# Recurrence's triangular inverse: products and copies of 32 instead of 64 columns from level 2 on

## The reference

```python
def step(state, inp):
    r_t, w_t, k_t, v_t, kk_t, a_t = inp
    sa = jnp.einsum('bhvk,bhk->bhv', state, kk_t)
    state = (state * w_t[:, :, None, :]
             - sa[..., None] * (kk_t * a_t)[:, :, None, :]
             + v_t[..., None] * k_t[:, :, None, :])
    return state, jnp.einsum('bhvk,bhk->bhv', state, r_t)
```

## Time and profile before

| | |
|---|---|
| median of 3 runs | 2653.7 us (2653.07 to 2654.84) |
| profiled execution | 2649.62 us, of which its span 2647.8 us |
| PE busy | 2543.0 us (96%), 18915 records |
| PE weight loads busy | 2117.9 us (80%) |
| DVE, ACT busy | 1655.8 us (63%), 1355.3 us (51%) |
| mean granted TensorE clock | 0.989 of full speed |
| recurrence of layer 0 | about 309 to 437 us of the span |
| recurrence of layer 1 | about 1088 to 1217 us of the span |

### The profile page before, as it was taken

The page is one execution under the profiler, slowest core; times in us unless marked ns, Lnnn a source line. Parts: engine busy times, 40 slices in busy tenths (PEclk is TensorE's granted clock), DMA queues, the critical chain, the costliest instruction groups (busy, mean ns, idle before and its releaser), DMA issues.

```text
span 2647.8 us, 46804 instructions
## 1 busy us (share of the span) xinstructions
PE 2543.0 (96%) x18915; PEld 2117.9 (80%) x18915; DVE 1655.8 (63%) x1905; ACT 1355.3 (51%) x1605; POOL 58.4 (2%) x94
## 2 busy tenths in 40 slices
PE   8999889999999999989999999988999999998998
PEld 6888577888888887577888888756998998876996
DVE  5546646765555556646765555687876776556774
ACT  5435434644444444334546445475674764456663
POOL 0002000000000002000000000000000000000000
PEclk9999999999999999999999999999999999999999
DMA  6547744645445449544555444402545555542453
GB/s 220 190 183 254 264 145 139 228 168 190 182 183 190 186 168 327 174 162 152 209 191 191 187 178 161 191 15 96 183 184 195 179 190 192 185 161 100 159 190 128
DMA packets 78315, 474.65 MB, mean 179 GB/s; under 512 B 9390, under 2 KB 13836, under 8 KB 27856
## 3 DMA queue, kind: packets, MB, share of 16 engines
q1 hardware_dynamic: 69088, 441.87, 45.7%
q0 software_dynamic: 7920, 29.58, 3.3%
q10 hardware_dynamic: 1152, 0.95, 0.2%
HBM read 463.68 MB, written 2.13 MB: 176 GB/s over the span
## 4 chain that ended last, share of the span: by engine, by line
PE 85%; DMA 5%; DVE 4%; ACT 3%; issue 1%; DVEq 1%; ACTq 0%; POOL 0%; SPq 0%
PE ACC L507 76%; DMA raw<-wstream 4%; PE MM L507 3%; PE TP L676 2%; DVE w_lo L1885 2%; PE TP L507 1%; ACT w_hi L1313 1%; DMA PREV<-V 1%; PE TP L1121 1%; DVE ST L2490 0%; PE ACC L880 0%; ACT ABT L1469 0%; DVE PR L2502 0%; DMA BIAS<-toe 0%; DVEq L2497 0%
## 5 line engine op out<-in xcount | busy, mean ns | idle before, releaser
L1885 DVE TENSOR_TENSOR w_lo<-raw,w_hi 128x2048 fp32r<-128x2048 f32 (+1 forms) x367 | 833.1, 2291 | 347.9 <-ACT w_hi L1313 332.7
L1313 ACT ACTIVATE w_hi<-raw 128x2048 fp32r<-128x2048 f32 (+1 forms) x367 | 691.6, 1902 | 431.3 <-DMA raw<-wstream 356.0
L507 PE MATMUL ACC<-w_hi,HA_hi 128*128 128x512 f32 (+2 forms) x1504 | 590.2, 393 | 8.3 <-DVE HA_lo L1968 3.9
L507 PE MATMUL ACC<-w_hi,HA_lo 128*128 128x512 f32 (+2 forms) x1504 | 583.1, 389 | 0.0
L507 PE MATMUL ACC<-w_lo,HA_hi 128*128 128x512 f32 (+2 forms) x1504 | 378.3, 388 | 0.1
L507 PEld LDWEIGHTS ACC<-w_hi,HA_hi 128*128 128x128 f32 x1504 | 284.1, 189 | 68.2 <-issue 11.3
L507 PEld LDWEIGHTS ACC<-w_hi,HA_lo 128*128 128x128 f32 x1504 | 284.3, 189 | 56.1
L507 PEld LDWEIGHTS ACC<-w_lo,HA_hi 128*128 128x128 f32 x1504 | 281.0, 188 | 58.3 <-DVE w_lo L1885 0.7
L507 PE MATMUL ACC<-HA_hi,w_hi 128*128 128x256 f32 x1056 | 256.8, 283 | 0.0
L507 PE MATMUL ACC<-HA_lo,w_hi 128*128 128x256 f32 x1056 | 256.6, 283 | 0.0
L507 PE MATMUL ACC<-w_hi,FT_hi 128*128 128x512 f32 x616 | 241.3, 392 | 0.0
(11 more groups left out here) (368 smaller groups left out, 3212.7 us busy)
## 6 DMA issues: line engine op xcount, KB each, us to landing
raw<-wstream SPq DMA_DIRECT2D x367, 1024.0 KB, 4.8
ADW<-wada SPq DMA_DIRECT2D x56, 512.0 KB, 3.9
ADW<-wada SPq DMA_DIRECT2D x20, 1024.0 KB, 14.8
BC<-vecs POOLq DMA_DIRECT2D x14, 512.0 KB, 7.2
BIAS<-toe SPq DMA_DIRECT2D x26, 128.0 KB, 2.8
BC<-mod_scr POOLq DMA_DIRECT2D x6, 512.0 KB, 4.9
MU<-mus POOLq DMA_DIRECT2D x2, 1280.0 KB, 11.8
WA<-lora POOLq DMA_DIRECT2D x2, 1024.0 KB, 10.1
```

The source lines that it names most:

```text
L507: return pe.matmul(*a, skip_group_check=True, **k)
L1313: act.activation(w_hi[:, s, 0:w], unit[:, 0:w], ACT.Copy).then_inc(sem["hi_ready"], 1)
L1885: dve.tensor_tensor(w_lo[:, s, 0:w], unit[:, 0:w], w_hi[:, s, 0:w].bitcast(F32), ALU.subtract).then_inc(sem["lo_ready"], 1)
```

## The change

- `XX` is laid out as two planes of eight heads (`[P, 2, 8, 64]`) instead of eight pairs (`[P, 8, 2, 64]`).
- `level_left` writes columns 256 to 511 of plane 0 of `INV[h]`, no longer 0 to 255, and `level` reads them there.
- From level 2 on, `level_left` moves and writes only the columns whose bit j is 0 (32 of 64, in runs of b = 4, 8, 16, 32), and `level_right` those with bit j 0 for the new X and those with bit j 1 for its transpose. The weights (`L`, `XX`, `TM`) stay 64 columns wide. The number of matmuls, of loads and of semaphore waits is the same.
- From level 2 on, `inverse` copies only those columns: 256 numbers a partition instead of 512, in runs of b. The rest of `XX` keeps what it had.
- Level 1, `first_inverse`, `left_inverse` and `final_inverse` keep their sizes. VectorE's mask still takes 256 numbers a partition; the columns that the left product didn't write hold the values of an earlier level, which the mask turns to zero off the diagonal.

```diff
-        XX, TM = ar("XX", 40, [P, 8, 2, CHUNK]), ar("TM", 44, [P, 8, CHUNK])
+        XX, TM = ar("XX", 40, [P, 2, 8, CHUNK]), ar("TM", 44, [P, 8, CHUNK])
...
+        def columns(v, j, bit):
+
+            return v.rearrange("p (k two b) -> p k two b", two=2, b=1 << j)[:, :, bit, :]
...
                     for ch, tok in enumerate(CHUNKS):
-                        last = mm(INV[h][tok if j == 1 else CHUNKS[1 - ch], 0, CHUNK * n:CHUNK * n + CHUNK],
-                                  L[tok, 4 * h + n, :], XX[tok, 4 * h + n, 0, :], start=True, stop=True)
+                        out_ = INV[h][tok if j == 1 else CHUNKS[1 - ch], 0, 256 + CHUNK * n:256 + CHUNK * n + CHUNK]
+                        x = XX[tok, 0, 4 * h + n, :]
+                        if j > 1:
+                            out_, x = columns(out_, j, 0), columns(x, j, 0)
+                        last = mm(out_, L[tok, 4 * h + n, :], x, start=True, stop=True)
                 last.then_inc(sem["t_ready"], 1)
...
             def level_right(l, i, j, h):
...
                         at = tok if j == 1 else across
-                        xt, tm = XX[at, 4 * h + n, 1, :], TM[at, 4 * h + n, :]
-                        mm(INV[h][tok, 0, CHUNK * n:CHUNK * n + CHUNK], xt, tm, start=True, stop=True)
-                        last = mm(INV[h][across, 1, CHUNK * n:CHUNK * n + CHUNK], tm, xt, start=True, stop=True)
+                        xt, tm = XX[at, 1, 4 * h + n, :], TM[at, 4 * h + n, :]
+                        new, new_t = (INV[h][rows, a, CHUNK * n:CHUNK * n + CHUNK] for a, rows in enumerate((tok, across)))
+                        tm_in, xt_in = tm, xt
+                        if j > 1:
+                            new, tm_in = columns(new, j, 0), columns(tm, j, 0)
+                            new_t, xt_in = columns(new_t, j, 1), columns(xt, j, 1)
+                        mm(new, xt, tm_in, start=True, stop=True)
+                        last = mm(new_t, tm, xt_in, start=True, stop=True)
                 last.then_inc(sem["u_ready"], 1)
...
-            def inverse(h):
+            def changed(v, j, apart):
+
+                b = 1 << j
+                return bass.AP(v.tensor, v.offset, [v.ap[0], [apart + b, 2], [2 * b, 128 // b], [1, b]])
+
+            def inverse(j, h):
+                dst, src = XX[:, :, 4 * h:4 * h + 4, :], INV[h][:, :, 0:256].rearrange("p a (n x) -> p a n x", n=4)
+                if j > 1:
+                    dst, src = changed(XX[:, 0, 4 * h, :], j, 512), changed(INV[h][:, 0, 0:CHUNK], j, 512)
                 act.wait_ge(sem["u_ready"], c.next("u_ready"))
-                act.activation(XX[:, 4 * h:4 * h + 4, :, :].rearrange("p n a x -> p a n x"),
-                               INV[h][:, :, 0:256].rearrange("p a (n x) -> p a n x", n=4),
-                               ACT.Copy).then_inc(sem["x_ready"], 1)
+                act.activation(dst, src, ACT.Copy).then_inc(sem["x_ready"], 1)

...
-                        inverse(h)
+                        inverse(j, h)
...
                 dve.wait_ge(sem["t_ready"], c.next("t_ready"))
-                tt(TM[:, 4 * h:4 * h + 4, :], four(INV[h][:, 0, 0:256]),
+                tt(TM[:, 4 * h:4 * h + 4, :], four(INV[h][:, 0, 256:512]),
                    mask(C_LEVEL + CHUNK * (j - 1), 4, CHUNK), ALU.mult).then_inc(sem["tm_ready"], 1)
```

More of the change, by code:

```diff
@@ L900, in first_inverse @@
                     for tok in CHUNKS:
-                        last = mm(LEFT[i][tok, 256 * h + CHUNK * n:256 * h + CHUNK * n + CHUNK], XX[tok, 4 * h + n, 1, :],
+                        last = mm(LEFT[i][tok, 256 * h + CHUNK * n:256 * h + CHUNK * n + CHUNK], XX[tok, 1, 4 * h + n, :],
                                   K_[tok, C_ID64:C_ID64 + CHUNK], start=True, stop=True)
@@ L931, in final_inverse @@
                         across = CHUNKS[1 - ch]
-                        last = mm(FINAL[n % 2][side(ch, n), place(n)], TM[across, n, :], XX[across, n, 1, :],
+                        last = mm(FINAL[n % 2][side(ch, n), place(n)], TM[across, n, :], XX[across, 1, n, :],
                                   start=True, stop=True)
@@ L1473, in left_inverse @@
                 act.wait_ge(sem["u_ready"], c.next("u_ready"))
-                act.activation(XX[:, 4 * h:4 * h + 4, 0, :], four(LEFT[i][:, 256 * h:256 * h + 256]), ACT.Copy) \
+                act.activation(XX[:, 0, 4 * h:4 * h + 4, :], four(LEFT[i][:, 256 * h:256 * h + 256]), ACT.Copy) \
                     .then_inc(sem["x_ready"], 1)
-            def inverse(h):
+            def changed(v, j, apart):
[5 more added lines that the diff above has]
+                    dst, src = changed(XX[:, 0, 4 * h, :], j, 512), changed(INV[h][:, 0, 0:CHUNK], j, 512)
                 act.wait_ge(sem["u_ready"], c.next("u_ready"))
-                act.activation(XX[:, 4 * h:4 * h + 4, :, :].rearrange("p n a x -> p a n x"),
-                               INV[h][:, :, 0:256].rearrange("p a (n x) -> p a n x", n=4),
-                               ACT.Copy).then_inc(sem["x_ready"], 1)
+                act.activation(dst, src, ACT.Copy).then_inc(sem["x_ready"], 1)
             def final_inverse():
@@ L2175, in low_grams @@
                 dve.drain()
-                tt(XX[:, 4 * h:4 * h + 4, 1, :], low, mask(C_PAIR_T, 4, CHUNK), ALU.mult).then_inc(sem["xt_ready"], 1)
+                tt(XX[:, 1, 4 * h:4 * h + 4, :], low, mask(C_PAIR_T, 4, CHUNK), ALU.mult).then_inc(sem["xt_ready"], 1)
             def other_grams(i, h):
```

## The result

The change makes the kernel slower. Its median is 2660.71 us over 13 executions (2649.85 to 2672.51), beside 2654.28 us over 13 executions of the kernel before on the same chip. The ratio is 1.0031, with a 95% interval of 1.0017 to 1.0045, or 4.5 to 12 us. 2660.7 lies just inside the upper end of the range, 2642 to 2661 us, and on the side, slower by more than 0.2%, that had a chance of 11%.

The account below looks back on a forecast made before the run. TensorE was taken to bound the kernel, with 85% of the chain. Gains of 1.28 + 0.22 + 0 = 1.5 us gave 2653.7 - 1.5 = 2652.2 us, range 2642 to 2661 us.

Parts of the forecast that it names:

- Step 1: ScalarE's copies from level 2: 383 instead of 597 ns, counted at six waits of TensorE for i = 0; 1.28 us gained.
- Rival D: ScalarE's copies: short runs eat the saving, so the change doesn't do what it says; 2653.5 us, chance 4%.
- Step 2: Last matmul of each group on the chain at i = 0: ends 27 ns sooner, eight times; 0.22 us gained.
- Step 3: Pace of left and right products: weight loads set it too, so halving moved columns gains 0 (bounds 0 and 26 us).
- rival A: Left and right products: weights don't set the pace, so fewer columns gain up to 27 us; 2627 us, chance 10%.
- Rival B: Products from level 2: broken runs of columns slow them, 19 us at three times the present price; 2671 us, chance 8%.
- Step 4: The rest, including left product's place, mask, layout, ScalarE's freed time and transfers: nothing added or gained on the chain.
- rival C: Gaps of TensorE's own list, one per layer: fewer (2647.6 or 2643 us, 6%) or more (2657 or 2661 us, 6%).

Follow-up runs that it names:

- e2: The change with products moving and writing all 64 columns again, keeping the layout and half copies; 2652.49 us, 0.9993 of the kernel before.
- e7: The whole change, but products from level 2 on move and write only 8 columns (other values computed); 2694.70 us, 1.0161 of the kernel before.
- e1: The change's layout and left products' own place alone, with products of 64 columns and whole copies; 2652.18 us, 0.9994 of the kernel before.
- e4: The whole change, but the products' 32 columns lie in one run (other values computed); 2667.75 us, 1.0047 of the kernel before.
- e3: The change without the short copies: layout and products of 32 columns, copies whole; 2665.14 us, 1.0044 of the kernel before.
- e8: The whole change plus two constant matmuls of 256 columns behind right h1 at i = 0, levels 2 to 4; 2662.26 us, 1.0047 of before.
- e10: The whole change, but products move 32 columns only for i = 1 to 3, 64 at i = 0; 2657.39 us, 1.0011 of the kernel before.

## Why the prediction was wrong

- **Step 1, the copies (1.28 us): right.** Line 1499 takes 383 ns with runs of 4, 8 and 16 numbers, 24 of 32 copies a tile, and the wait ahead of left h0 fell by 0.22 us in e2. Rival D is out.
- **Step 2, the last matmul (0.22 us): the size was right, the place wrong.** Records with 32 columns were to last about 191 ns. Records of the left products of half 0 in i = 0 at the full clock, with 64 (before), 32 (after) and 8 columns (e7), ns as in the earlier trace rows:

```profile
L507 PE MATMUL ACC<-XX,L x48: 218/218/267, 321.4 to 328.1; 64*64 64x64 f32 x48
...
L511 PE MATMUL ACC<-XX,L x48: 219/219/241, 323.8 to 330.0; 64*64 64x32 f32 x48
...
L511 PE MATMUL ACC<-XX,L x18: 199/199/220, 318.1 to 320.4; 64*64 64x8 f32 x18
```

  The usual record, and with it the last of a group, lasts 219 ns beside 218: nothing is gained there. What got shorter is the start of a group behind a wait: its first record lasts 240 instead of 267 ns, and the next pair of records starts 79 instead of 107 ns after it. (The 186 ns in the row of `XX` above are the shortest of 640 records.) Those are the 27 ns of step 2. The round of the ring from level 2 to 3 shows the sum of both steps: 2.35 instead of 2.62 us is 0.27 less, and 0.214 + 2 x 0.027 = 0.268. The profile's ends of matmuls are modelled, so the distance between starts is the firmer reading. i = 0 as a whole can't show 0.75 us a layer: the same 625 records of layer 0, all at a clock of 1.00, took 26.8 us in before (307.2 to 334.0), 26.2 in after (309.8 to 336.0), and 27.4 in e1, which has nothing shortened. What the Trainium skill (TensorEngine Tiling, Instruction Overhead) says, that one free column has the latency of 60, is borne out for 32 against 64 by the usual record, 219 and 218 ns, and not by the first of a group; with 8 columns the usual record is 20 ns shorter.
- **Step 3, the pace (0 us): right where it was worked out, and the forecast failed here all the same.** A left group takes 0.46 or 0.47 us with 64, 32 and 8 columns at the full clock, so rival A is out. Rival B is out too: broken runs (after) and one run of 32 (e4) give a loss of the same order, 1.0031 and 1.0047, and stages that read alike. The slowdown by non-contiguous PSUM patterns that the Trainium skill (SBUF — State Buffer, SBUF: two separate sides) speaks of doesn't show in this case. What I didn't ask is what it means for TensorE to keep the pace and move half as much. I took every duration of this step from rows at the full clock and multiplied by a count, as if the clock would stay what it was.
- **Step 4, the rest, and rival C: this is the step that failed.** Step 4 put the clock of the stage at nothing without a reason: its list named waits, queues, layout and transfers. The clock appears only in rival C, behind a gap of TensorE's own list, as 3.5 us at 0.58, or 1.5 us a gap, and C asked only whether there would be more or fewer gaps. The two gaps stayed (2.28 and 3.45 us in after, beside 3.04 and 3.17 in the earlier trace rows). What changed is the time at the lower level: some 49 us of the two stages instead of 8, about 14 of the difference at those same gaps, 7 behind a stop of 1.52 us, and 20 in i = 0 of layer 1. The stages took 12.2 us more. No chance was given to that mechanism. That the time fell inside the range was luck: the range reached 2661 for more gaps, which didn't come.

What the runs show is that the products with fewer moved columns bring the loss, and that the granted clock falls with them (64, 32 and 8 columns: clock 0.987, 0.982 and 0.962; ratio 1, 1.0031 and 1.0161). The number of matmuls and of loads was the same in all three, and neither the layout (e1), the copies (e2) nor broken runs (e4) made the difference. What the chip itself looks at stays open. So does why one execution of the same kernel falls and another doesn't, what the gaps of TensorE's list are, and why left and right products together lose more than both apart.

## What to carry to other kernels

Where moved columns don't set TensorE's pace, as in these 64x64 products in fp32, moving fewer of them buys no pace, and it can cost the clock of the stage: look at the granted clock of each stage before pricing such an edit, and write down what the stage would be worth at the lower level. When a stage gets longer and every part of it got shorter, read the windows of that stage with their clock first, before any wait. TensorE's count of busy microseconds didn't tell here whether its clock would hold.

## What the hardware did that I had not expected

- TensorE's clock fell to 1.2 GHz in the middle of work with no wait over 0.25 us: 6.05 of 6.70 us busy ahead of it (e3). It stayed there while TensorE was busy for 19.85 of 20.60 us (after, from 1106.20).
- At the gaps of TensorE's list the lower level lasted 3.4 us in both layers of before (3.4 and 6.8 in e1 and e2), 13.7 and 6.8 us in after, and 13.7 in both layers of e8 and e10.
- The less was moved, the slower: 8 of 64 columns cost 43 us, and the stages ran at a clock of 0.76 and 0.74.
- With two constant matmuls a level, 256 columns each, the clock stood at 1.00 through i = 0 in both layers of the profile of e8 (without them in 2 of 10 such stretches), and then it fell elsewhere.
- A 64x64 record in fp32 lasts 218 ns with 64 moving columns and 219 with 32. The first of a group behind a wait lasts 240 instead of 267 ns.
- ScalarE takes 383 ns for 256 numbers from PSUM whether they lie there in one piece (line 1474) or in runs of 4, 8 and 16 (line 1499 of after).
